# Attention scores from three rounded products, and half of a row combination on GpSimd, in a two-block fp32 transformer kernel

## What is computed

```python
s = jnp.einsum('bqhmd,bkhmd->bhmqk', qb, kk).astype(jnp.float32) * scale
p = jax.nn.softmax(s, axis=-1)
p = p[:, :, 0] - lam_full * p[:, :, 1]
return jnp.einsum('bhqk,bkhe->bqhe', p.astype(vv.dtype), vv)
...
o = rmsnorm_2(o, subln_g) * (1.0 - lam_init)
return o.reshape(B, n, D_MODEL) @ wo
```

## Time and profile before

| | |
|---|---|
| median of 3 runs | 2507.63 us (2507.43 to 2507.78) |
| span of the profiled execution | 2508.3 us |
| PE busy | 2474.0 us, 99% of the span |
| DVE busy | 1507.2 us, 60% |
| ACT busy | 990.5 us, 39% |
| POOL busy | 136.8 us, 5% |
| granted TensorE clock | 0.997 over the span, 1.00 in the attention |
| attention units | first scores at 1423.6 us, last h_lo of the heads at 1560.9 us |

### The profile page before, as it was taken

The page is one execution under the profiler, slowest core; times in us unless marked ns, Lnnn a source line. Parts: engine busy times, 40 slices in busy tenths (PEclk is TensorE's granted clock), DMA queues, the critical chain, the costliest instruction groups (busy, mean ns, idle before and its releaser), DMA issues.

```text
span 2508.3 us, 32888 instructions
## 1 busy us (share of the span) xinstructions
PE 2474.0 (99%) x13466; PEld 2067.1 (82%) x13466; DVE 1507.2 (60%) x2618; ACT 990.5 (39%) x1997; POOL 136.8 (5%) x148
## 2 busy tenths in 40 slices
PE   8999999999999999999999999999999999999998
PEld 6878888778888788888888988888888888888887
DVE  8787753555666557766664288676654644633434
ACT  5543242454355442333522377432223423422222
POOL 1000000000010010000122000100000001000001
PEclk9999999999999999999999999999999999999999
DMA  4221012212333144654212100366632222222222
GB/s 148 84 85 35 18 52 87 99 68 70 132 135 120 66 178 175 229 208 151 93 67 85 51 1 15 137 229 227 222 114 86 106 100 91 95 101 101 96 85 72
DMA packets 39944, 270.36 MB, mean 108 GB/s; under 512 B 4337, under 2 KB 4593, under 8 KB 9073
## 3 DMA queue, kind: packets, MB, share of 16 engines
q1 hardware_dynamic: 30064, 206.71, 23.2%
q0 software_dynamic: 9040, 60.33, 6.7%
q10 hardware_dynamic: 688, 1.22, 0.2%
HBM read 266.14 MB, written 2.10 MB: 107 GB/s over the span
## 4 chain that ended last, share of the span: by engine, by line
PE 93%; DVE 4%; ACT 2%; DMA 0%; issue 0%; SPq 0%; DVEq 0%; ACTq 0%
PE bank L142 91%; PE bank L145 2%; DVE w_lo L151 1%; ACT tmp L148 0%; DVE dd L151 0%; DVE x_t L159 0%; DMA w_raw<-in_pack_gates 0%; ACT w_hi L148 0%; DVE tmp L151 0%; DVE change L159 0%; ACT L148 0%; DVE first_lo L159 0%; DVE dd L145 0%; DVE da_stat L168 0%; DVE low L151 0%
## 5 line engine op out<-in xcount | busy, mean ns | idle before, releaser
L142 PE MATMUL bank<-h_hi,w_hi 128*128 128x512 f32 x1824 | 694.5, 395 | 0.1
L142 PE MATMUL bank<-h_lo,w_hi 128*128 128x512 f32 x1824 | 677.1, 390 | 0.0
L151 DVE TENSOR_TENSOR w_lo<-w_raw,w_hi 128x512 fp32r<-128x512 f32 (+3 forms) x746 | 490.2, 712 | 143.5 <-ACT w_hi L148 143.0
L142 PE MATMUL bank<-h_hi,w_lo 128*128 128x512 f32 x1824 | 570.8, 390 | 0.0
L148 ACT ACTIVATE w_hi<-w_raw 128x512 fp32r<-128x512 f32 (+3 forms) x746 | 426.5, 637 | 308.0 <-PE bank L142 293.8
L142 PEld LDWEIGHTS bank<-h_lo,w_hi 128*128 128x128 f32 x1824 | 342.2, 188 | 72.3 <-DVE h_lo L159 0.8
L142 PEld LDWEIGHTS bank<-h_hi,w_hi 128*128 128x128 f32 x1824 | 342.5, 188 | 70.3 <-issue 0.8
L142 PEld LDWEIGHTS bank<-h_hi,w_lo 128*128 128x128 f32 x1824 | 341.5, 188 | 68.1
L142 PE MATMUL bank<-f_hi,w_hi 128*128 128x512 f32 x816 | 315.6, 390 | 0.2 <-DVE w_lo L151 0.2
L142 PE MATMUL bank<-f_lo,w_hi 128*128 128x512 f32 x816 | 300.1, 389 | 0.0
L142 PE MATMUL bank<-f_hi,w_lo 128*128 128x512 f32 x816 | 270.3, 389 | 0.0
(11 more groups left out here) (383 smaller groups left out, 3110.7 us busy)
## 6 DMA issues: line engine op xcount, KB each, us to landing
w_raw<-in_pack_ffn SPq DMA_DIRECT2D x60, 1024.0 KB, 4.8
ada_w<-in_ada_w POOLq DMA_DIRECT2D x48, 1024.0 KB, 5.1
w_raw<-in_pack_mlp SPq DMA_DIRECT2D x32, 1024.0 KB, 4.8
w_raw<-in_pack_gdn_qkv SPq DMA_DIRECT2D x12, 1024.0 KB, 4.7
w_raw<-in_pack_sc_cu SPq DMA_DIRECT2D x8, 1024.0 KB, 4.8
w_raw<-in_pack_ffn SPq DMA_DIRECT2D x8, 768.0 KB, 4.1
w_raw<-in_pack_gdn_z SPq DMA_DIRECT2D x4, 1024.0 KB, 4.7
w_raw<-in_pack_gate_a SPq DMA_DIRECT2D x4, 1024.0 KB, 4.7
```

Source lines behind the costliest of these rows:

```text
L142: return self.engine.matmul(*a, **k) if self.engine is not None else self
L151: return self.engine.tensor_tensor(*a) if self.engine is not None else self
```

## The change

- `scores` makes three fp32r products per piece: rounded q by rounded k, the rest of q by rounded k, rounded q by the rest of k. Twelve matmuls stand where four float32 ones stood.
- `parts_of_head` on GpSimd makes the four parts of a head, one instruction each (piece 0: `da_k_hi`, 1: `da_k_lo`, 2: `da_q_hi`, 3: `da_q_lo`). Heads 0 and 1 are split right behind the rotary embedding; piece (n+6) mod 4 of head (n+6)/4 follows unit n, for heads 2 to 7.
- `combine` is cut in two: DVE keeps the weight and the right 384 columns (one instruction), GpSimd makes the left 384 in two dependent instructions (a product, then a sum in place).
- turn and values are moved one unit later on PE, turned on ACT; DVE's square_sum too.
- result(0) to result(6) go from ACT to DVE.
- Small tiles move to space that lives longer; the rest of k takes the place of `k_all`.

The diff stands without its lines that only name or move tiles, and without one of the waits that the next sentence names. `exps(n)` waits for `pool_da probs(n-2)` and `tops(n)` for `pool_da probs(n-3)`, each beside the wait on `dve_da` that it had.

```diff
@@ -3017,6 +3023,26 @@
 
+    def parts_of_head(G, h, piece):
+        i = h % 2
+        if piece == 0:
+            if h < 2:
+                G.wait_ge(*at("dve_da", ("rope", rope_number("q", h))))
+                G.wait_ge(*at("act_da", ("k", h)))
+            else:
+                G.wait_ge(*at("pe_da", ("scores", NCH * (h - 1) - 1)))
+            G.tensor_copy(da_k_hi[i][:, :], k_all[:, h, :]).then_inc(*up("pool_da", ("k_hi", h)))
+        elif piece == 1:
+            G.wait_ge(*at("pool_da", ("k_hi", h)))
+            G.tensor_tensor(da_k_lo[:, h, :], k_all[:, h, :], da_k_hi[i][:, :].bitcast(F32), ALU.subtract).then_inc(
+                *up("pool_da", ("k_lo", h)))
+        elif piece == 2:
+            G.tensor_copy(da_q_hi[i][:, :], da_q[:, h, :]).then_inc(*up("pool_da", ("q_hi", h)))
+        else:
+            G.wait_ge(*at("pool_da", ("q_hi", h)))
+            G.tensor_tensor(da_q_lo[i][:, :], da_q[:, h, :], da_q_hi[i][:, :].bitcast(F32), ALU.subtract).then_inc(
+                *up("pool_da", ("q_lo", h)))
+
     def context_scalar(S):
@@ -3070,10 +3096,13 @@
             rope_pool(G, "q", n)
+        for h in range(2):
+            for piece in range(4):
+                parts_of_head(G, h, piece)
 
     def context_made(lane):
         all_of(lane, ("pe_tile", ("da_v", 0, V_PANELS - 1, V_LATE - 1)), ("act_da", ("v", V_PANELS - 1, V_LATE - 1)),
-               ("dve_da", ("rope", 2 * DT - 1)), ("pool_rope", 2 * DT - 1))
+               ("dve_da", ("rope", 2 * DT - 1)), ("pool_da", ("q_lo", 1)))
 
@@ -3091,14 +3120,30 @@
             cut, place = slice(m * P, (m + 1) * P), score_banks(n)
-            (q0, q1), (k0, k1) = ([a[64 * mp:64 * mp + 64] for mp in range(2)] for a in (da_q[:, h, cut], k_all[:, h, :]))
+            q_hi, q_lo, k_hi, k_lo = da_q_hi[h % 2][:, cut], da_q_lo[h % 2][:, cut], da_k_hi[h % 2], da_k_lo[:, h, :]
+            pairs = ((q_hi, k_hi), (q_lo, k_hi), (q_hi, k_lo))
+
+            def product(mp, part, a, b):
+                rows, (q, k) = slice(64 * mp, 64 * mp + 64), pairs[part]
+                return T_.matmul(place[:, mp, a:b], q[rows, :], k[rows, a:b], start=(part == 0), stop=(part == 2))
+
             if n >= 2:
                 T_.wait_ge(*at("act_da", ("exp", n - 2, 1)))
-            T_.matmul(place[:, 0, 512:NK], q0, k0[:, 512:NK], start=True, stop=True).then_inc(*up("pe_da", ("narrow", n)))
-            T_.matmul(place[:, 1, 256:NK], q1, k1[:, 256:NK], start=True, stop=True)
-            T_.matmul(place[:, 0, 0:512], q0, k0[:, 0:512], start=True, stop=True)
+            if m == 0:
+                T_.wait_ge(*at("pool_da", ("q_lo", h)))
+            product(0, 0, 512, NK)
+            product(1, 0, 256, NK)
+            product(0, 1, 512, NK)
+            product(1, 1, 256, NK)
+            product(0, 2, 512, NK).then_inc(*up("pe_da", ("narrow", n)))
+            product(0, 0, 0, 512)
+            product(1, 2, 256, NK)
+            product(0, 1, 0, 512)
             T_.wait_ge(*at("pe_da", ("narrow", n)))
-            T_.matmul(place[:, 1, 0:256], q1, k1[:, 0:256], start=True, stop=True).then_inc(*up("pe_da", ("scores", n)))
+            product(1, 0, 0, 256)
+            product(0, 2, 0, 512)
+            product(1, 1, 0, 256)
+            product(1, 2, 0, 256).then_inc(*up("pe_da", ("scores", n)))
 
@@ -3107,7 +3152,7 @@
                 T_.wait_ge(*at("act_da", ("turned", n - 1, 1)))
-            T_.wait_ge(*at("dve_da", ("probs", n)))
+            T_.wait_ge(*at("dve_da", ("probs", n)) if half else at("pool_da", ("probs", n)))
             for j in range(HALF_KT):
@@ -3117,7 +3162,7 @@
             if m == 0 and h > 0:
-                T_.wait_ge(*at("act_da", ("out", h - 1)))
+                T_.wait_ge(*at("dve_da", ("out", h - 1)))
             T_.wait_ge(*at("act_da", ("turned", n, 1)))
@@ -3153,12 +3198,14 @@
             Ring.holder[bank] = holder
-        for n in range(2, len(UNITS)):
-            scores(n)
-            turn(n - 2, 0)
-            if n >= 3:
-                values(n - 3)
-            turn(n - 2, 1)
+        scores(2)
+        for n in range(3, len(UNITS) + 1):
+            if n < len(UNITS):
+                scores(n)
+            turn(n - 3, 0)
+            if n >= 4:
+                values(n - 4)
+            turn(n - 3, 1)
         turn(LAST - 1, 0)
@@ -3177,12 +3224,11 @@
                 S.wait_ge(*at("dve_da", ("probs", n - 2)))
+                S.wait_ge(*at("pool_da", ("probs", n - 2)))
             S.wait_ge(*at("dve_da", ("top", n)))
             for mp, total in enumerate((da_first[:, h, m:m + 1], s[:, 2:3])):
-                if mp and n >= 2:
-                    turned(n - 2, 1)
-                if mp and n >= 6 and n % 4 == 2:
-                    result(n // 4 - 1)
+                if mp and n >= 3:
+                    turned(n - 3, 1)
                 S.activation(p[:, mp, :], score_banks(n)[:, mp, :], ACT.Exp, bias=s[:, mp:mp + 1], scale=-1.0,
@@ -3216,13 +3262,13 @@
                     take_values(S, V_PANELS - 1, m)
-            if 2 <= n < len(UNITS) + 2:
-                turned(n - 2, 0)
+            if n >= 3:
+                turned(n - 3, 0)
             if n < len(UNITS):
                 exps(n)
-            elif n < len(UNITS) + 2:
-                turned(n - 2, 1)
-            if n == len(UNITS):
+            else:
+                turned(n - 3, 1)
+            if n == len(UNITS) + 1:
                 S.activation(spare_col, param("eps"), ACT.Sqrt)
@@ -3257,13 +3304,18 @@
             V.wait_ge(*at("dve_da", ("weight", n)))
-            V.scalar_tensor_tensor(d[:, :], p[:, 1, :], s[:, 4:5], p[:, 0, :], ALU.mult, ALU.add).then_inc(
+            right = slice(HALF_KT * P, NK)
+            V.scalar_tensor_tensor(d[:, right], p[:, 1, right], s[:, 4:5], p[:, 0, right], ALU.mult, ALU.add).then_inc(
                 *up("dve_da", ("probs", n)))
+
+        def result(h):
+            V.wait_ge(*at("pe_da", ("out", 4 * h + 3)))
+            V.tensor_copy(da_q[:, h, :], out_bank).then_inc(*up("dve_da", ("out", h)))
 
         def square_sum(u):
             h, m = UNITS[u]
             part = da_q[:, h, m * P:(m + 1) * P]
-            V.wait_ge(*at("act_da", ("out", h)))
+            V.wait_ge(*(at("act_da", ("out", h)) if h == DA_H - 1 else at("dve_da", ("out", h))))
             if u:
@@ -3300,9 +3352,11 @@
                 combine(n - 1)
-            if n >= 7:
-                square_sum(n - 7)
-        for u in range(len(UNITS) - 6, NCH * (DA_H - 1)):
+            if n >= 8:
+                square_sum(n - 8)
+            if n >= 7 and n % 4 == 3:
+                result(n // 4 - 1)
+        for u in range(len(UNITS) - 7, NCH * (DA_H - 1)):
             square_sum(u)
@@ -3329,6 +3383,22 @@
     def attend_pool(G):
+        def combine(n):
+            s, p, d = da_stat[n % 3], da_p[n % 2], da_diff[n % 2]
+            left = slice(0, HALF_KT * P)
+            if n >= 2:
+                G.wait_ge(*at("pe_da", ("turned", n - 2, 0)))
+            G.wait_ge(*at("dve_da", ("weight", n)))
+            G.tensor_scalar(d[:, left], p[:, 1, left], s[:, 4:5], None, ALU.mult).then_inc(*up("pool_da", ("weighted", n)))
+            G.wait_ge(*at("pool_da", ("weighted", n)))
+            G.tensor_tensor(d[:, left], d[:, left], p[:, 0, left], ALU.add).then_inc(*up("pool_da", ("probs", n)))
+
+        context_made(G)
+        for n in range(len(UNITS)):
+            combine(n)
+            h, piece = divmod(n + 6, NCH)
+            if 2 <= h < DA_H:
+                parts_of_head(G, h, piece)
         residual_pool(G, "da_o", 0, ffn_sum[0])
```

More of the change, by code:

```diff
@@ L117 @@
     "dve_gated", "dve_merged", "dve_gla", "dve_xa", "dve_mlp", "dve_ada", "dve_da", "dve_ffn", "dve_sc", "dve_out")
-POOL_SIGNALS = ("pool_sum", "pool_pad", "pool_gdn", "pool_gla", "pool_rope")
+POOL_SIGNALS = ("pool_sum", "pool_pad", "pool_gdn", "pool_gla", "pool_rope", "pool_da")
 LOADS = ("raw_loaded0", "raw_loaded1", "prm_loaded", "consts_loaded", "x_loaded0", "x_loaded1", "x_loaded2",
@@ L287, in build_program @@
     spare_col, two_cols = prm_whole[:, N_PARAMS:N_PARAMS + 1], prm_whole[:, N_PARAMS + 1:N_PARAMS + 9]
+    with ExitStack() as st:
+        da_stat = [sb(st, f"da_stat{i}", [P, 8]) for i in range(3)]
+        da_first, da_sums, da_root = (sb(st, f"da_{n}", [P, DA_H, NCH]) for n in ("first", "sums", "root"))
+        da_gain = sb(st, "da_gain", [P, 1])
     rstd = sb(top, "rstd", [P, T])
+    with ExitStack() as st:
+        da_q_hi, da_q_lo = ([sb(st, f"da_q_{part}{i}", [P, T], F32R) for i in range(2)] for part in ("hi", "lo"))
     tmp = [sb(top, f"tmp{i}", [P, T]) for i in range(4)]
@@ L368, in build_program @@
     with ExitStack() as st:
-        k_all = sb(st, "da_k", [P, DA_H, NK])
+        with ExitStack() as s2:
+            k_all = sb(s2, "da_k", [P, DA_H, NK])
+        da_k_lo = sb(st, "da_k_lo", [P, DA_H, NK], F32R)
         v_all = sb(st, "da_v", [P, KT, D])
@@ L381, in build_program @@
         da_pt = [sb(st, f"da_pt{i}", [P, KT, P]) for i in range(2)]
```

(5 more changed lines are left out.)

## The result

The changed kernel takes 2518.04 us (median of 5, 2516.97 to 2519.58) against 2507.63, a ratio of 1.0042 [1.0031 to 1.0053]: 10.4 us slower. Its profiled execution has a span of 2516.1 us.

What follows compares the result with a forecast made beforehand. PE was taken to bound the attention stage, with DVE close behind. Start -0.6, units +4.0 and tail +0.9 made +4.3 us, from a median of 2507.63 to a forecast of 2512 us, range 2501 to 2524.

Steps and rivals of the forecast that it cites:

- the likeliest case: Attention stage: GpSimd holds up DVE, which takes PE's place as bound; 2506.5 to 2519 us, chance 0.56.
- my own upper bound: GpSimd's product at the two-input price, 0.97 us: four units take 16.6 us, about +15, 2522 us.
- Scores' slot 1.25, unit 3.40: PE, attention: fp32r scores take 1.25 us instead of 1.49, a gain of 0.24; PE's unit falls to 3.40.
- rival 3: PE scores: the fp32r row halves run one after the other, unit 4.43 us, +23, 2531 us; chance 0.04.
- VectorE's half combination 0.62, result 0.62: DVE: 384 columns of the combination take 0.62 us, 0.40 less; a head's result takes 0.62, one unit in four.
- GpSimd's product 0.65: GpSimd's one-input product over 384 columns takes 0.65 us, priced between a memset and two inputs.
- rival 2: GpSimd blocks square_sum over product and sum, or its product costs a two-input price: 2522 to 2528 us; chance 0.21.
- square_sum waits for the product: DVE: square_sum, held up by GpSimd's product, ends at 1.29 instead of 0.85 us; next minimum starts at 1.36, not 0.94.
- That would fit if GpSimd were alone: GpSimd's own work was put at 11.9 us a head, 3.0 a unit, before meetings with DVE.
- the thinnest place: PE at a new head: scores, waiting for the rest of q, still finish before the minimum wants them, by 0.2 us.
- Moving turn and values a unit back adds no instruction: PE, attention: running turn and values one unit later was taken to add no instruction; no cost was given.
- My tail of +0.9: End of attention: the last square sums end 2.9 us behind the last weight instead of 2.0, delaying the norm: +0.9.

Runs made afterwards that it cites:

- result_act: The changed kernel with the heads' results back on ScalarE (ACT) instead of VectorE: 2516.78 us, ratio 1.0039.
- copy_for_product: The changed kernel with GpSimd's product by the weight (384 columns) replaced by a plain copy, multiplication left out: 2524.86 us, ratio 1.0071.
- cut_128: The changed kernel with the combination cut at column 128 instead of 384, so GpSimd makes 128 columns and VectorE 640: 2508.70 us, ratio 1.0008.
- no_pieces: The changed kernel without the parts of heads 2 to 7; all heads use those of heads 0 and 1: 2506.97 us, ratio 1.0000.
- squares_first: The changed kernel with VectorE's square sum ahead of its half combination instead of behind it: 2521.17 us, ratio 1.0056.
- parts_earlier: The changed kernel with each part of a head made one unit earlier on GpSimd: 2516.30 us, ratio 1.0034.
- lag_two: The changed kernel with turning and values one unit earlier again, two units behind: 2568.54 us, ratio 1.0246.

## Why the prediction came out as it did

The sign, the size class and the place were right: slower, within the likeliest case's range of 2506.5 to 2519, and all of it in the attention stage. The mechanism was half right, and two terms that were wrong pulled against each other: the product was far dearer than taken (4), and VectorE's square sum never waited for it (5). The sum was +4.3 us against +10.4 measured, and that 2518 lies within the case's range is in part luck: my own upper bound, with the product at 0.97, already gave +15, and the product costs 1.24.

1. *PE is the bound before and stops being it.* Right: 92.8 of 104 us busy, against all of it.
2. *Scores' slot 1.25, unit 3.40.* Mis-sized: the slot is 1.34 to 1.36 and the unit 3.51. Both row halves do run at once (rival 3 is out), but the second pair of matmuls starts 0.22 behind the first, where I took 0.12 for the first weight load. The gain is 0.13 instead of 0.24.
3. *VectorE's half combination 0.62, result 0.62.* Right where nothing meets it: 0.62, up to 1.16 beside a part. The result takes 0.68, which costs nothing (result_act).
4. *GpSimd's product 0.65.* The term that failed worst: 1.24 alone, nearly twice, and more than the two-input sum over the same columns (1.00). My upper bound, "two inputs", was 0.97, so the value lies outside both of my ends. That I took a memset as the nearest relative of a product with a scalar from SBUF was the wrong row to lean on. The casts went the other way: 0.61 and 0.83 instead of 0.87 and 1.31. In all GpSimd's own work is 4 x (1.24 + 1.00) + 0.83 + 1.83 + 0.61 + 1.27 = 13.5 us a head instead of 11.9. Of rival 2, the premise (a product over 0.8) came true, but not its course: GpSimd doesn't keep the port against square_sum in after. It does in copy_for_product, which came out at 2524.9, within that rival's 2522 to 2528.
5. *square_sum waits for the product, and so the minimum starts 0.42 later.* Wrong in after: all 22 of its records in 1440 to 1544 us are 0.277 to 0.287. VectorE's two instructions go first and the product waits for both, 1.67 instead of 1.24 at the median. The delay is thus GpSimd's: 1.9 us a head on top of 13.5 make 15.4 of the 16.05 us of a head. In copy_for_product the delay does fall on square_sum, behind the sum and not behind the first instruction, and costs more.
6. *"That would fit if GpSimd were alone", 15.17 us for four units.* It came to 16.05. GpSimd is now what a head waits for most, then the weight that is late by a meeting (1.56 instead of 0.22 for the small product), then the head's start.
7. *Scores of a new head covered by 0.2 us, "the thinnest place".* The cover was not there: 0.83 us of wait at each head. It was named as a sign of being wrong, and it was one; making the parts a unit earlier gave back 1.5 us in all.
8. *Moving turn and values a unit back adds no instruction.* True, and the wrong question: it adds 2.4 us behind the last unit. My tail of +0.9 came from the square sums and missed that.
9. *The sum.* Start -0.6, measured -0.9 (first scores to fourth minimum, 14.0 to 13.1). Units +4.0, measured +8.2 (fourth to last minimum, 102.1 to 110.3). Tail +0.9, measured +2.4 (last minimum to last h_lo, 21.3 to 23.7). Together +4.3 against +9.8.

What made the kernel slower is then: parts that start while VectorE reads two operands from SBUF, and a GpSimd chain of 13.5 us plus 1.9 of waiting per head, which is longer than the 14.0 us that PE needs for it. Neither alone is shown to be the cause of after's unit. Without the parts it is 3.51, with fewer columns 3.58, and with less GpSimd work but worse meetings 4.21. What each would be worth in after with the other gone was not separated; nor were the parts placed in after itself, or cut_128 with placed parts, tried.

## What to carry to other kernels

Try to put work given to GpSimd beside VectorE instructions that read PSUM (here the minimum over 1536 columns, 1.76 us), by the wait that starts it: that one wait was worth 16.4 us here, more than any choice of which engine does how much. Look at each pair of instructions that meets, not only at busy time: a GpSimd that was three quarters idle made VectorE the bound, and shortening its instruction made the kernel slower. And count what a software pipeline's extra stage leaves to do behind its last step.

## What the runs showed of the hardware

- GpSimd over 128 partitions in float32: product with a column scalar 1.24 us for 384 columns and 0.60 for 128; sum of two tensors 1.00 for 384 and 0.45 for 128; copy 0.51 for 384; cast to fp32r 0.61 for 512 and 0.83 for 768; subtraction into fp32r 1.27 and 1.83. At 384 columns the product with a scalar is thus the dearest, and a copy the cheapest by half.
- Copy, casts, sum and subtractions hold up VectorE instructions with two operands in SBUF, the custom square sum (0.28 to 1.09) and the product of one column (0.22 to 1.56) too. The blocked one pays what is left of the other's length, less 0.13 us (square sum) or 0.2 (the others). The Trainium skill's page SBUF — State Buffer (section "Who interferes with whom") states the contention for a GpSimd instruction that reads SBUF, and these runs agree, which decides the question that my prediction had left open for one-input work.
- The same section says that issue order, and not the form of the instruction, decides who blocks. With the half combination recorded 0.07 us or more ahead, GpSimd's product waits for it (1.54 to 1.78 us). With the product recorded 0.05 us or more ahead it goes first, at its own 1.24, and the combination is the longer one. GpSimd's copy goes first though recorded 0.02 to 0.03 us behind. So order in the records decides these, but for starts closer than some 0.05 us.
- The product doesn't hold the port for its whole length. In the eight cases of after, no_pieces, result_act, squares_first and parts_earlier where the half combination started 0.05 to 0.35 us behind it, the combination ended 0.98 to 1.00 us behind the product's start, a quarter of a microsecond before the product's own end. In copy_for_product it ended 0.92 us behind the start of the copy, which takes 0.51 in all: the product, at 1.24, held VectorE up hardly longer than the copy. The shortest distance, in parts_earlier:

```profile
1535.22 1.24 POOL L154 TENSOR_SCALAR da_diff<-da_p,da_stat 128x384 f32<-128x384 f32 x1 [0.66 <-DVE da_stat L159]
1535.27 0.94 DVE L159 SCALAR_TENSOR_TENSOR da_diff<-da_p,da_stat 128x384 f32<-128x384 f32 x1 [0.22 <-PE bank L145]
```

- One case stays open. In after the product, at work or waiting since 1488.65, is also passed by square_sum, which starts 0.47 us later; in copy_for_product GpSimd's sum, waiting since 0.25 us before square_sum, is not. That the scalar operand makes the difference fits, but is argued and not shown.
- Three-product fp32r scores on 64 rows in both row halves: 12 matmuls in 1.34 to 1.36 us, against 1.49 for the 8 in float32.
- A stretch with PE busy for 0.52 of 3.05 us was followed by 3.55 us at the 1.2 GHz level (lag_two). From 1440 to 1540 us that run's mean granted clock is 0.80, in a stage where before and after show 1.00.
